# Attention in a two-layer trunk: probabilities scaled on ScalarE, S5 arguments spread over four splits, one widening product two units later

## What is computed

```python
q = rmsnorm(q, q_gain); k = rmsnorm(k, k_gain)            # per head of 64
scores = einsum(qc, kb) * HEAD_DIM ** -0.5                # chunks of 64 frames, a band of 128 keys
m = maximum(max(scores), sink)
p = exp(scores - m)
denom = sum(p) + exp(sink - m)
o = einsum(p / denom, vb)
```

## Time and profile before

| | |
|---|---|
| median of 3 runs | 1994.78 us (1992.68 to 1995.01) |
| the profiled execution | 1994.46 us |
| its span, first to last instruction | 1992.7 us |
| mean granted clock of TensorE | 0.996 |
| busy: PE, DVE, ACT, POOL | 98%, 63%, 45%, 32% |

### The profile page before, as it was taken

One profiled execution on the slowest core, in us unless ns is written; L12 is line 12 of the kernel. 1 busy time (PEld: TensorE's weight loads), 2 busy tenths in 40 slices (PEclk: granted clock), 3 DMA queues, 4 the chain that ended last, 5 costly groups with the idle time before them and its releaser, 6 DMA issues.

```text
span 1992.7 us, 31567 instructions
## 1 busy us (share of the span) xinstructions
PE 1955.5 (98%) x11578; PEld 1651.4 (83%) x11578; DVE 1257.0 (63%) x1394; ACT 906.1 (45%) x1190; POOL 647.2 (32%) x858
## 2 busy tenths in 40 slices
PE   8999999999999999999997999999999999999999
PEld 7778788888888888888877888888888888888887
DVE  6886757755765576567549655576556556645654
ACT  6456655443444344344453544544344434434442
POOL 3483339787777788540009400000000000000000
PEclk9999999999999999999998999999999999999999
DMA  7544477666766666776788666655666666666654
GB/s 225 179 118 134 165 201 205 197 217 206 225 205 222 199 224 204 225 252 201 254 284 283 196 190 181 196 181 190 192 182 200 194 193 184 196 191 189 193 194 162
DMA packets 285583, 400.19 MB, mean 201 GB/s; under 512 B 23329, under 2 KB 185265, under 8 KB 283409
## 3 DMA queue, kind: packets, MB, share of 16 engines
q1 hardware_dynamic: 278032, 371.77, 59.5%
q0 software_dynamic: 5216, 24.52, 3.9%
q10 hardware_dynamic: 2208, 2.11, 0.3%
HBM read 371.87 MB, written 25.17 MB: 199 GB/s over the span
## 4 chain that ended last, share of the span: by engine, by line
PE 88%; DVE 5%; ACT 2%; POOL 1%; issue 1%; DMA 1%; SPq 0%; ACTq 0%; DVEq 0%; POOLq 0%
PE ps L728 25%; PE ps L729 12%; PE ps L680 12%; PE ps L682 12%; PE ps L681 12%; DVE Wl L1574 2%; PE px L1060 1%; PE px L1058 1%; PE px L1059 1%; PE ps L1058 1%; PE ps L1060 1%; PE ps L1059 1%; PE px L944 1%; ACT Wh L1159 1%; PE ps L665 1%
## 5 line engine op out<-in xcount | busy, mean ns | idle before, releaser
L1574 DVE TENSOR_TENSOR Wl<-raw,Wh 128x1024 fp32r<-128x1024 f32 x660 | 838.4, 1281 | 620.8 <-ACT Wh L1159 618.0
L1159 ACT ACTIVATE Wh<-raw 128x1024 fp32r<-128x1024 f32 x660 | 691.0, 1057 | 748.3 <-PE ps L682 379.4
L728 PE MATMUL ps<-A,Wh 128*128 128x512 f32 x2364 | 832.9, 397 | 3.7 <-DVE A L1661 2.1
L729 PE MATMUL ps<-A,Wl 128*128 128x256 f32 x2364 | 658.5, 279 | 0.0
L728 PEld LDWEIGHTS ps<-A,Wh 128*128 128x128 f32 x2364 | 444.3, 188 | 111.1 <-issue 4.7
L729 PEld LDWEIGHTS ps<-A,Wl 128*128 128x128 f32 x2364 | 445.4, 188 | 0.3
L680 PE MATMUL ps<-Wh,A 128*128 128x512 f32 x1024 | 399.8, 390 | 0.0
L682 PE MATMUL ps<-Wh,A 128*128 128x512 f32 x1024 | 398.5, 389 | 0.0
L681 PE MATMUL ps<-Wl,A 128*128 128x512 f32 x1024 | 398.4, 389 | 0.0
L682 PEld LDWEIGHTS ps<-Wh,A 128*128 128x128 f32 x1024 | 192.2, 188 | 40.3
L680 PEld LDWEIGHTS ps<-Wh,A 128*128 128x128 f32 x1024 | 192.2, 188 | 40.1
(11 more groups left out here) (377 smaller groups left out, 2033.3 us busy)
## 6 DMA issues: line engine op xcount, KB each, us to landing
raw<-in_w_up_dram SPq DMA_DIRECT2D x256, 512.0 KB, 3.9
raw<-in_w_down_dram SPq DMA_DIRECT2D x256, 512.0 KB, 4.0
raw<-in_w_glu_dram SPq DMA_DIRECT2D x64, 512.0 KB, 3.7
raw<-in_w_in_e_dram SPq DMA_DIRECT2D x52, 512.0 KB, 3.9
raw<-in_w_out_e_dram SPq DMA_DIRECT2D x32, 512.0 KB, 4.1
s_params<-stg POOLq DMA_DIRECT2D x16, 1024.0 KB, 6.1
slot<-s_params SPq DMA_DIRECT2D x12, 768.0 KB, 7.7
slot<-s_params SPq DMA_DIRECT2D x12, 256.0 KB, 7.5
```

Source lines behind the costliest of these rows:

```text
L728: mm(ps[:, b + t, :], Wh[:, s, c, cols], A[:, k, :], start=(n == 0), stop=False)
L729: last = mm(ps[:, b + t, 0:L], Wl[:, s, c, cols], A[:, k, 0:L], start=False, stop=(n == KC - 1))
L1159: fn(Wh[:, s], raw[:, s], ACT.Copy).then_inc(hi_split, 1)
L1574: tt(Wl[:, s], raw[:, s], Wh[:, s].bitcast(F32), ALU.subtract).then_inc(lo_split, 1)
```

## The change

1. DVE's `softmax_norm` ends with the reciprocal and raises a new semaphore `sum_inverse`. ACT has a new `softmax_scaled(i)`: four copies of `pb` onto itself, with the reciprocal as the scale, at unit 9+2i, ahead of `softmax_exp(i+1)`. They raise `probs`.
2. `s5_arguments` has its 20 instructions spread: 4 after the first split, 8 after the second, 4 after the third, 4 (and the old one) after the fourth.
3. The last `widen` moves from unit 5 to unit 7, its `normed` on DVE from unit 6 to unit 8.

```diff
@@ tensor: beside(n)
-                if n == SLOT_Q:
+                if n == SLOT_Q + 2:
                     pe.wait_ge(kd_ready, 1)
                     widen(LC - 1, 7).then_inc(qk_wide, 1)
@@ scalar
+            def softmax_scaled(i):
+                d = i % 2
+                act.wait_ge(sum_inverse, i + 1)
+                for n in range(NCH):
+                    nk = P if n else CH
+                    last = fn(pb[:, d, n, 0:nk], pb[:, d, n, 0:nk], ACT.Copy, scale=am[:, d, 4, n:n + 1])
+                last.then_inc(probs, 1)
+
@@ scalar: beside(n)
                 i, odd = divmod(n - ATT0, 2)
+                if odd and 0 <= i - 1 < LC:
+                    softmax_scaled(i - 1)
                 if odd and 0 <= i < LC:
                     softmax_exp(i)
@@ vector: s5_arguments(part)
+                def turns(out_, turn):
+
+                    link(ts(tmp, hb, TWO_PI_INV, turn, ALU.mult, ALU.add))
+                    link(ts(tmp, tmp, MAGIC, None, ALU.add))
+                    link(ts(tmp, tmp, -MAGIC, None, ALU.add))
+                    link(stt(out_, tmp, -PI_HI, hb, ALU.mult, ALU.add))
+
+                def reduced(out_, turn):
+
+                    link(stt(out_, tmp, -PI_MID, out_, ALU.mult, ALU.add))
+                    link(stt(out_, tmp, -PI_LO, out_, ALU.mult, ALU.add))
+                    link(ts(out_, out_, 2.0 * math.pi * turn, None, ALU.add))
+                    link(ts(out_, out_, -PI_CLAMP, PI_CLAMP, ALU.max, ALU.min))
+
                 if part == 0:
...
-                    for out_, turn in ((s2, 0.0), (c2, 0.25)):
-
-                        link(ts(tmp, hb, TWO_PI_INV, turn, ALU.mult, ALU.add))
...
+                if part == 1:
+                    turns(s2, 0.0)
+                    reduced(s2, 0.0)
+                if part == 2:
+                    turns(c2, 0.25)
                 if part == 3:
+                    reduced(c2, 0.25)
@@ vector: softmax_norm(i)
                 link(tt(am[:, d, 4, :], am[:, d, 2, :], am[:, d, 3, :], ALU.add))
-                link(nc.vector.reciprocal(am[:, d, 4, :], am[:, d, 4, :]))
-                tt(pb[:, d, 0, 0:CH], pb[:, d, 0, 0:CH], am[:, d, 4, 0:1].to_broadcast([P, CH]), ALU.mult)
-                tt(pb[:, d, 1:NCH], pb[:, d, 1:NCH], am[:, d, 4, 1:NCH].unsqueeze(2).to_broadcast([P, NCH - 1, P]),
-                   ALU.mult).then_inc(probs, 1)
+                nc.vector.reciprocal(am[:, d, 4, :], am[:, d, 4, :]).then_inc(sum_inverse, 1)
@@ vector: beside(n)
-                if n == SLOT_Q + 1:
+                if n == SLOT_Q + 3:
                     dve.wait_ge(qk_wide, 2)
                     normed(LC - 1, 7).then_inc(q_normed, 1)
```

More of the change, by code:

```diff
@@ L317, in trunk_kernel @@
         probs = sem("probs")
+        sum_inverse = sem("sum_inverse")
         p_t = sem("p_t")
```

## The result

The changed kernel takes 1984.1 us (median of 5 runs, 1983.01 to 1986.8) where the kernel before takes 1994.78 (5 runs beside them). The ratio is 0.995, with a 95% interval of 0.994 to 0.9961: 10 us faster, between 7.8 and 12. The forecast was 1988.0 us and its range began at 1985.5, so the sign was right and the gain came out larger than the range allowed. The profiled execution took 1983.94 us, its span is 1982.2 us.

The account below looks back on a forecast made before the run. PE, busy 98%, could gain only in its gaps or slow-clock stretches, with VectorE late in the attention loop. Terms 1.3 + 0.6 + 1.2 + 1.4 + 0.7 + 1.5 = 6.7 us gave 1988.0 us; range 1985.5 to 1992.0.

Parts of the forecast that it names:

- S5 arguments: Between VectorE's splits in the S5 arguments: the second split starts 3.7 us earlier, so PE's wait goes; gain 1.3 us.
- The last head's root: At unit 5: the widening product no longer stands behind the keys, so PE's wait goes; gain 0.6 us.
- The first head: Before the first transposes: inverse 0.4 us later, probabilities ready at 116.4 us as before, so the 1.37 us gap stays.
- The passes: Later heads: two products of 1.43 us leave VectorE's loop, 8.69 us a pass becomes 7.26, under PE's 8.03.
- gap of 1.62: PE's idle time until 121.47 us, before value products: the second head's exponentials start earlier; gain 1.2 us.
- three later gaps: PE's other three waits before value products go as the lag shrinks from head to head; gain 1.4 us.
- the gates: PE's wait before the first gate products, which was for the last exponentials, goes; gain 0.7 us.
- the clock: PE's 3 us at granted clock 0.50, from 123 to 126 us, return to full clock; gain 1.5 us.
- Rival A: The clock stays: it falls behind the 1.37 us gap or where it did; 5.2 us gained, 1989.5 us; chance 0.24.
- Rival B: VectorE's held-up time, 0.65 us a product, moves to the next instruction; gain 3.5 us, 1991.1 us; chance 0.16.
- Rival C: ScalarE's four copies lengthen the loop: 2003 us at 4.2 us a head, slower from about 3.0 us; chance 0.03.
- D: Only the S5 arguments and last head's root gain, the heads' gaps all stay; 1992.6 us; chance 0.07.

Follow-up runs that it names:

- the run with 3.08: The changed kernel with ScalarE's scaling cut into fourteen copies of 32 elements a head, in place of one of 64 and three of 128; measured 1995.69 us (ratio 1.0005).

## Why the prediction came out as it did

- *S5 arguments, 1.3 us*: right; 1.41 in the piece by the first profile of before, PE without a wait.
- *The last head's root, 0.6 us*: mis-sized at the keys (0.81), and its price has the wrong sign. The step that failed is "now stands ahead of the first head's sum", carried into the next part as "plus 0.4": the later work was counted as a delay of the first head. Alone on the kernel before, the root's move made the first head 0.47 us shorter. Measured against PE, which is earlier too, the head's chain starts 0.36 us earlier; the root takes that back, but VectorE's instructions fell differently beside GpSimd's, half a microsecond shorter in all. This last part was not to be foreseen from the rows shown, and in that sense it is luck.
- *The first head, "the 1.37 us stay"*: wrong, and by that same 0.4. The price of the copies was right. Without the 0.4 the prediction's count gives 115.97 us (114.72 + 1.25), and with the scaling alone the copies ended at 115.88 and PE's transposes started at 115.93, with a gap of 0.95. In the whole change the gap is 0.73. Counted as nothing, the first head gained 0.69.
- *The passes*: 1.2 (gap of 1.62), 1.4 (three later gaps), 0.7 (the gates) and 1.5 (the clock), 4.8 in all; measured 5.83 and 5.77. The gaps went entirely. The clock's term was wrong as a mechanism: the slow stretch is absent in a second profile of the same kernel, at the same length of the passes, with 1.3 us more of idle time before the value products. That the sum of the four came near is luck in this sense: the term stood for idle time that the first profile did not show. What the four together stand for is the loop's excess over PE's 8.03 us.
- *A gap costs more than it shows*: with 0.60 shown the keys' piece lost 0.81; in the second profile of before the passes hold 4.3 and 0.6 us of waits, 4.9, and 5.7 went. Seven waits, 0.8 us: about 0.1 each. This was in none of the terms, which were taken from shown idle time.
- *Rival A* ("the clock stays") could not have been told from the forecast by its price, since a slow stretch costs nothing under slack. *Rival B* was right that held-up time moves and wrong about what it costs. VectorE's split did take on some of it, 1472 to 1618 ns on average from 96 to 180 us, but with the products gone the loop had room for it. *Rival C*'s boundary of 3.0 us fits the run with 3.08, 1.2 us slower than before with an interval that holds no change. *D* did not come.

The touched pieces are 8.75 us where the sum had 6.7: 0.7 more at the first head, 1.0 in the passes, 0.2 at the keys and 0.1 at the S5 arguments. From the profiled execution of before that gives 1985.7 us, inside the range. What carried the time below it is the remaining 1.3 us or so. A part of it can be the S5 piece, which was short in the first profile of before: the two second profiles differ by 8.97 us in the touched pieces, and from the 1993.89 us beside them that gives 1984.9, 0.6 above the measured 1984.29. The intervals allow that nothing remains (8.7 lies within 7.8 to 12), but both measurements of the changed kernel lie on the same side, and no stage of the profiles shows it: this stays open.

## What to carry to other kernels

Where the pace is set by a loop of other engines, the main engine's idle time and its slow clock are two faces of the same excess: compare start-to-start times of the same instruction with what the main engine needs, and do not add the two. When something leaves the loop, let the chain run forward from its new start, also what starts earlier, not only what was added. And before an instruction is moved between engines, ask whether it is late because of its work or because another engine shuts it out: here either remedy took out nearly the same gaps, and together they were worth less than 1 us more in the touched pieces.

## What the runs showed of the hardware

- A VectorE instruction on four numbers took 0.15 or 0.16 us with GpSimd out of its way and up to 1.26 us beside one of its instructions, its end within 0.02 us of GpSimd's in the three cases above. The Trainium skill (SBUF — State Buffer, section "Who interferes with whom") says that a VectorE instruction with two SBUF inputs and a GpSimd one that reads SBUF contend, and that whoever issues first holds the shared ports for the whole instruction; the traces agree. The page also counts scalings and copies among those that can be shut out, where they run in a two-port mode. That fits the scaled maxima, one tensor from SBUF, at 1.26 us, and the 0.96 us at 117.31 in the earlier trace rows, which ended at 118.27 when GpSimd's instruction ended at 118.24; the mode itself stands in no trace. The reductions, which read PSUM, took 0.19 to 0.23 and 0.54 to 0.56 us in every kernel.
- TensorE's clock fell for some 3 us behind a gap of 1.62 us in one profile of the kernel before and stayed at 1.00 behind the same gap in the other. In the kernel with fourteen copies it fell behind a gap of 2.80 us (two rows); in the one with the products behind the maxima it stayed at 1.00 through a gap of 3.33 us, the longest of all, which ended at 118.64 (the row behind them):

```profile
112.00:114.00 2.00, 0.00 (x0) 0.00 (x0) 1.97 (x3) 2.00 (x11) 1.84 (x3) 1.00 0.61 213
114.00:116.00 2.00, 1.57 (x7) 1.48 (x8) 0.58 (x1) 2.00 (x12) 2.00 (x2) 0.55 0.07 11
```

```profile
116.00:118.00 2.00, 0.00 (x0) 0.00 (x0) 1.97 (x4) 1.69 (x10) 1.92 (x3) 1.00 0.56 198
```

  So in these kernels the length of a gap alone, from 1.6 to 3.3 us, did not say whether the clock fell.
- A copy on ScalarE from SBUF onto itself with a column as its scale took 390 ns for 128 elements and 347 for 64, and neighbours overlap: seven of 64 elements took 1.78 us, fourteen of 32 took 3.08.
